# Sums of squares as a rounded pair, tiles turned by transposes, and a rearranged start in a ten-block transformer kernel

## The reference

```python
def norm_mod(h, j):
    shift = mod[:, j, 0][:, None, :]
    scale = mod[:, j, 1][:, None, :]
    return _rms(h) * g_norm[l, j] * (1.0 + scale) + shift

x = x + 0.5 * gate(0) * _swiglu(norm_mod(x, 0), w_ffn_up[l, 0], w_ffn_down[l, 0])
x = x + gate(1) * _mixer(norm_mod(x, 1), w_in[l], ...)
```

## Time and profile before

| | |
|---|---|
| three runs | 1594.5, 1595.07, 1602.45 us; median 1595.07 |
| profiled execution | 1595.17 us |
| its span, first to last instruction | 1593.2 us |
| busy | TensorE 1559.0 us, VectorE 1285.0, ScalarE 906.3, GpSimd 243.0 |
| mean granted TensorE clock | 0.998 of 2.4 GHz |

### The profile page before, as it was taken

One profiled execution on the slowest core, in us unless ns is written; L12 is line 12 of the kernel. 1 busy time (PEld: TensorE's weight loads), 2 busy tenths in 40 slices (PEclk: granted clock), 3 DMA queues, 4 the chain that ended last, 5 costly groups with the idle time before them and its releaser, 6 DMA issues.

```text
span 1593.2 us, 32431 instructions
## 1 busy us (share of the span) xinstructions
PE 1559.0 (98%) x13288; PEld 1536.6 (96%) x13288; DVE 1285.0 (81%) x1933; ACT 906.3 (57%) x1565; POOL 243.0 (15%) x256
## 2 busy tenths in 40 slices
PE   4999999999999999999999999999999999999998
PEld 3999999999999999999999999999999999999998
DVE  6788898888888888888887898778888889786553
ACT  5455457665554655459664445567555466664553
POOL 4122000022210222000112231001221010021100
PEclk9999999999999999999999999999999999999999
DMA  9999974559998899864569998434999973457761
GB/s 347 338 339 331 328 272 158 160 188 348 310 318 280 290 306 322 308 222 151 185 224 340 311 317 288 159 115 147 311 333 339 317 235 121 142 188 238 240 213 41
DMA packets 110996, 403.11 MB, mean 253 GB/s; under 512 B 12562, under 2 KB 12818, under 8 KB 110720
## 3 DMA queue, kind: packets, MB, share of 16 engines
q1 hardware_dynamic: 109280, 395.87, 72.0%
q0 software_dynamic: 1568, 5.17, 1.1%
HBM read 399.94 MB, written 1.05 MB: 252 GB/s over the span
## 4 chain that ended last, share of the span: by engine, by line
PE 87%; DVE 8%; ACT 2%; DMA 1%; issue 1%; SPq 0%; DVEq 0%; ACTq 0%
PE PS L557 86%; DVE SCR L1692 2%; DVE WL L1689 2%; DMA ring<-in_ada 1%; DVE SCR L1689 1%; DVE ring L1715 1%; ACT WH L1211 1%; DVE SCR L2046 1%; DVE SMALL L2045 1%; DVE SMALL L2084 0%; ACT SCR L1497 0%; PE PS L1050 0%; DVE SCR L1686 0%; DVE MOD L1686 0%; ACT HH L1243 0%
## 5 line engine op out<-in xcount | busy, mean ns | idle before, releaser
L1689 DVE TENSOR_TENSOR WL<-ring,WH 128x1024 fp32r<-128x1024 f32 (+1 forms) x508 | 603.9, 1222 | 186.4 <-ACT WH L1211 186.1
L557 PE MATMUL PS<-HH,WH 128*128 128x256 f32 (+1 forms) x2640 | 629.0, 280 | 2.2 <-ACT WH L1211 2.2
L557 PE MATMUL PS<-HL,WH 128*128 128x256 f32 (+1 forms) x2640 | 614.9, 277 | 0.0
L1211 ACT ACTIVATE WH<-ring 128x1024 fp32r<-128x1024 f32 (+1 forms) x508 | 511.0, 1049 | 44.3 <-PE PS L557 42.3
L557 PEld LDWEIGHTS PS<-HH,WH 128*128 128x128 f32 x2640 | 496.7, 188 | 3.3 <-ACT WH L1211 2.3
L557 PEld LDWEIGHTS PS<-HL,WH 128*128 128x128 f32 x2640 | 491.6, 188 | 0.6
L557 PE MATMUL PS<-HH,WL 128*128 128x256 f32 (+1 forms) x2640 | 375.9, 278 | 0.8 <-DVE WL L1689 0.6
L1715 DVE CUSTOM_DVE_ANT_0 ring<-ring,CB,VC 128x1024 f32<-128x1024 f32 x238 | 331.0, 1407 | 11.3 <-DMA ring<-in_ada 11.3
L557 PEld LDWEIGHTS PS<-HH,WL 128*128 128x128 f32 x2640 | 337.1, 189 | 1.6 <-DVE WL L1689 1.6
L557 PE MATMUL PS<-AH,WH 128*128 128x256 f32 x1056 | 291.9, 276 | 0.0
L557 PE MATMUL PS<-AH,WL 128*128 128x256 f32 x1056 | 291.6, 276 | 0.2 <-DVE WL L1689 0.2
(11 more groups left out here) (215 smaller groups left out, 1474.9 us busy)
## 6 DMA issues: line engine op xcount, KB each, us to landing
ring<-in_up SPq DMA_DIRECT2D x176, 512.0 KB, 5.5
ring<-in_ada SPq DMA_DIRECT2D x144, 512.0 KB, 6.1
ring<-in_ffn SPq DMA_DIRECT2D x132, 512.0 KB, 4.8
ring<-in_mod SPq DMA_DIRECT2D x96, 512.0 KB, 5.9
ring<-in_down SPq DMA_DIRECT2D x88, 512.0 KB, 5.9
ring<-in_win SPq DMA_DIRECT2D x64, 512.0 KB, 5.5
ring<-in_wout SPq DMA_DIRECT2D x32, 512.0 KB, 4.2
ring<-in_winv SPq DMA_DIRECT2D x8, 512.0 KB, 4.4
```

Of the source, the lines that this page charges most:

```text
L557: return e.matmul(out, lhsT, rhs, start=start, stop=stop, skip_group_check=skip)
L1211: e.activation(half_of(i)[0], slot_of(("half", i, 0))[:, 0:w], ACT.Copy).then_inc(s_hi, 1)
L1689: return e.tensor_tensor(out, a, b, op)
```

## The change

- **Squares.** GpSimd now adds all eight squares (seven steps). ScalarE rounds the sum into `SH`, GpSimd writes the remainder into `SL` (both lie where chunks 0 and 1 of `SQ` were), and TensorE sums over partitions by two fp32r products with rounded ones (`onesr`). They stand behind `early(n, 1)` instead of inside `early(n, 0)`. On ScalarE one ring half, rounded after R before, is rounded before Ln.
- **Tiles.** VectorE scales the tile itself in place (`unit_rows`, 128x256) instead of the identity, and TensorE turns it by two transposes.
- **c.** The first transfer into `CB` is gone; TensorE turns the eight columns of silu(c), each spread over 128 columns, into PSUM, and ScalarE copies the result into `CB`. The second c is still a transfer.
- **Start.** Eight fp32 products of X by the identity, whose result nobody reads, stand before the first weight product.
- **Mixer 1.** `stick_weights(1)` stands before `hi(u0 + 11)`.

```diff
 def square_sums(m):
-    for c in range(1, KD - 1):
+    for c in range(1, KD):
         e.wait_ge(s_sq, 8 * m - 7 + c)
         if c > 1:
-            e.wait_ge(s_psum, 6 * m + c - 7)
+            e.wait_ge(s_psum, 7 * m + c - 8)
         e.tensor_tensor(SQ[:, c, :], SQ[:, c - 1, :], SQ[:, c, :], ALU.add).then_inc(s_psum, 1)
+    e.wait_ge(s_sqh, m)
+    e.tensor_tensor(SL[:, :], SQ[:, KD - 1, :], SH[:, :].bitcast(F32), ALU.subtract).then_inc(s_sql, 1)
 ...
 def sum_squares(m):
-    e.wait_ge(s_psum, 6 * m)
+    e.wait_ge(s_sql, m)
     if m > 1:
         e.wait_ge(s_r, m - 1)
-    mm(PS[:, 6, 0:256], ones, SQ[:, KD - 2, :], start=True, stop=False)
-    e.wait_ge(s_sq, 8 * m)
-    mm(PS[:, 6, 0:256], ones, SQ[:, KD - 1, :], start=False, stop=True).then_inc(s_ss, 1)
+    mm(PS[:, 6, 0:256], onesr[:, :], SH[:, :], start=True, stop=False)
+    mm(PS[:, 6, 0:256], onesr[:, :], SL[:, :], start=False, stop=True).then_inc(s_ss, 1)
 ...
     if p == 0:
-        sum_squares(n)
         k = KD - 1
 ...
     last.then_inc(s_half, 1)
+    if p == 1:
+        sum_squares(n)
 ...
-        last = mm(PS[:, turn_bank(n, o), 256 + 128 * c:384 + 128 * c], OT[o % 4][:, 128 * c:128 * c + 128], DG[o % 2])
+        last = e.transpose(PS[:, turn_bank(n, o), 256 + 128 * c:384 + 128 * c], OT[o % 4][:, 128 * c:128 * c + 128], ident1)
 ...
 e.wait_ge(s_const, 16)
+e.wait_ge(s_cc, 1)
+for k in range(KD):
+    last = e.transpose(PS[:, k // 4, 128 * (k % 4):128 * (k % 4) + 128], vec("c", k).to_broadcast([128, 128]), ident)
+last.then_inc(s_cspread, 1)
 e.wait_ge(s_xload, 16)
 ...
 last.then_inc(s_flip, 1)
+for c in range(8):
+    mm(PS[:, 6, 0:256], ident, X[:, c % KD, :])
 ...
 def norm(m):
+    e.wait_ge(s_psum, 7 * m)
+    e.activation(SH[:, :], SQ[:, KD - 1, :], ACT.Copy).then_inc(s_sqh, 1)
+    hi_half(2 * UNIT0[m] + 3)
     e.wait_ge(s_ss, m)
     step(e.activation(R[:, :], PS[:, 6, 0:256], ACT.Ln, bias=eps, scale=1.0 / D))
     e.activation(R[:, :], R[:, :], ACT.Exp, scale=-0.5).then_inc(s_r, 1)
-    hi_half(2 * UNIT0[m] + 3)
 ...
                 tile_scale(n, o0 + 1)
+                stick_weights(1)
                 hi(u0 + 11)
-                stick_weights(1)
 ...
-e.wait_ge(s_cload, 16)
-e.activation(CB[:, :], CB[:, :], ACT.Silu).then_inc(s_cb, 1)
 lnexp()
+e.wait_ge(s_cspread, 1)
+e.activation(CB[:, :], PS[:, 0:2, :].rearrange("p a s -> p (a s)"), ACT.Copy).then_inc(s_cb, 1)
 ...
-def diagonal(n, o):
+def unit_rows(n, o):
+
     e.wait_ge(s_oss, o + 1)
-    if o >= OUT0[n] + 2:
-        e.wait_ge(s_ot, o - 1)
-    ts(DG[o % 2], ident1, SM_[:, 114 + o % 2:115 + o % 2], None, ALU.mult, None).then_inc(s_od, 1)
+    ts(OT[o % 4], OT[o % 4], SM_[:, 114 + o % 2:115 + o % 2], None, ALU.mult, None).then_inc(s_od, 1)
```

More of the change, by code:

```diff
@@ L181, in vec @@
             return VC[:, VEC[name] + i:VEC[name] + i + n]
-        ident, ones, bd, ntri, partner, rev, causal, nones = (const(n) for n in (
-            "ident", "ones", "bd", "ntri", "partner", "rev", "causal", "nones"))
+        ident, bd, ntri, partner, rev, causal, nones = (const(n) for n in (
+            "ident", "bd", "ntri", "partner", "rev", "causal", "nones"))
         eps = const("eps")
-        ident1 = identr[:, :].bitcast(F32)
+        ident1, ones1 = identr[:, :].bitcast(F32), onesr[:, :].bitcast(F32)
         one = const("one")
@@ L279, in build @@
         JK = scr(256)
-        DG = [scr(128) for _ in range(2)]
         Scratch.at = 0
@@ L872, in recurrence_sums @@
                     for k in range(4):
-                        last = mm(PS[:, 7, 0:256], ones, GT[:, k, :], start=k == 0, stop=k == 3)
+                        last = mm(PS[:, 7, 0:256], ones1, GT[:, k, :], start=k == 0, stop=k == 3)
                     last.then_inc(s_gnss, 1)
@@ L986, in latent_sums @@
                             mm(PS[:, 6, 256 + t:257 + t], MSQ[:, k, 128 * t:128 * t + 128], one, start=k == 0, stop=k == 1)
-                    mm(PS[:, 6, 0:256], ones, MSQ[:, 2, :]).then_inc(s_mss, 1)
+                    mm(PS[:, 6, 0:256], ones1, MSQ[:, 2, :]).then_inc(s_mss, 1)
                 def keys():
@@ L1992, in mixer1 @@
                 share(n, 2)
-                diagonal(n, o0)
-                diagonal(n, o0 + 1)
+                unit_rows(n, o0)
+                unit_rows(n, o0 + 1)
                 lo(u0 + 11)
@@ L2005, in mixer1 @@
                 partial(n, 3)
-                diagonal(n, o0 + 2)
-                diagonal(n, o0 + 3)
+                unit_rows(n, o0 + 2)
+                unit_rows(n, o0 + 3)
                 lo_half(2 * u0 + 24)
@@ L2178, in mixer2 @@
                 tile_rest(n, o0 + 2)
-                diagonal(n, o0 + 4)
+                unit_rows(n, o0 + 4)
                 gates(n)
@@ L2189, in mixer2 @@
                 partial(n, 1)
-                diagonal(n, o0 + 5)
+                unit_rows(n, o0 + 5)
                 maxima2(a0 + 5, 1)
@@ L2195, in mixer2 @@
                 tile_rest(n, o0 + 4)
-                diagonal(n, o0 + 6)
+                unit_rows(n, o0 + 6)
                 partial(n, 3)
@@ L2202, in mixer2 @@
                 tile_rest(n, o0 + 5)
-                diagonal(n, o0 + 7)
+                unit_rows(n, o0 + 7)
                 partial(n, 5)
```

28 lines of the change are left out of this document (15 added, 13 removed).

## The result

| | changed | before |
|---|---|---|
| median of 15 runs each | 1604.54 us | 1596.53 us |
| lowest and highest | 1594.09, 1614.59 | 1593.82, 1604.05 |
| ratio of the changed kernel to before | 1.0047, 95% interval 1.0029 to 1.0065 | |
| profiled execution, its span | 1606.41, 1604.6 us | 1595.17, 1593.2 us |

The forecast was 1589.8 with a range up to 1594.0: it failed, on the side of slower. Besides the median, the spread is to be noted: 20 us between runs of one and the same changed kernel, 10 us before.

What follows compares the result with a forecast made beforehand. TensorE, busy 98% of the span, was taken to bound the kernel; gains of 1.7 (start), 1.4 (boundaries), 0.6 and 1.7 (mixers) sum to 5.4 us, so 1595.2 - 5.4 = 1589.8 us, range 1583.5 to 1594.0.

Steps and rivals of the forecast that it cites:

- What bounds the kernel: Whole kernel: TensorE is busy 98% of the span, so time falls only where its queue gets shorter or waits less.
- A wait also costs some 0.1 on the next spacing.: At the boundaries: besides its 0.3 us length, TensorE's wait adds some 0.1 us to the step after it.
- The start: Before and in the first half-column: first weight product still at 34.65, its 24 products faster, gain 1.7 us.
- The clock part: At the start: clock at 2.4 GHz, so the first half-column's 24 products take 2.75 us instead of 4.45.
- the prediction's rule that transposes do not count as work for the clock: At the start: the eight new transposes warm nothing for TensorE's clock; the real products do; no change in time.
- The boundary: Nine sub-block changes: 0.63 us saved each, 0.2 left after waits; 1.4 us at seven, -0.15 each at two.
- The spare of the sum: At the boundary: the sum's input is ready at 329.5, TensorE arrives at 330.26, 0.7 us spare; 2 after an FFN.
- rival (c): At nine boundaries the sum's input SL comes too late; every microsecond costs 9, 1607.8 at 2 us; chance 0.06.
- Mixers: Mixer ends, tiles turned by transposes: 0.3 us gained per first-type mixer, 0.85-0.9 per second-type; 0.6 and 1.7 in all.
- (a): Whole kernel: all savings count, other engines are never late; 13.4 us gained, so 1581.8; chance 0.15.
- (b): At the start: no gain, as transfers are not sooner or the clock drops; 1591.5 to 1593; chance 0.2.
- four signs of being wrong: TensorE waiting for SL; no gap before the eighth product; clock 0.50 after 31; VectorE idle above 0.5 us before early products.

Runs made afterwards that it cites:

- f1: The changed kernel run again with nothing edited: median 1597.03 us of eleven runs, one of 4037.51 standing apart; ratio 1.0004.
- e7: The kernel before with three chained, unread VectorE instructions ahead of the remainders of h at each boundary: 1611.85 us, ratio 1.0098.
- e9: e5's kernel with c spread by a transfer again, without the eight transposes: 1593.19 us, +1.3.
- e10: e5's kernel without the eight unread products by the identity: 1593.2 us, +1.3.
- e2: The changed kernel with one 256-column product given as two of 128 in each sub-block after the first: 1596.36 us, ratio 0.9985.
- e5: The changed kernel with two split products (256 columns as 128 and 128) in every FFN, twelve in all: 1591.91 us, ratio 0.9962.
- f3: e1's kernel with two split products in sub-block 0 and two 258-column products in each of the other five FFNs: 1598.45 us, ratio 0.9996.
- e12: e4's kernel with the twelve split products of e5: 1593.0 us, +1.1 to e5.
- e3: The kernel before with one unread VectorE instruction of 0.4 us ahead of the remainders of h at each boundary: 1596.33 us, ratio 0.9999.
- e4: The changed kernel with the squares, their sum and its place as before: 1590.71 us, ratio 0.9972.
- e8: The kernel before with the twelve split products of e5: 1597.92 us, ratio 1.0001.
- e1: The changed kernel with the squares summed by one plain fp32 product inside the second early half-column, without SH and SL: 1599.86 us, ratio 1.0011.

## Why the prediction was wrong

Point by point:

- **What bounds the kernel.** Right: TensorE at 98%, its queue alone counts. But I took the time of a product as a constant, 0.114 us. This is the step that failed, and it is in no single term: every term of the sum multiplies or subtracts at that one rate. In the profile of after 1463, 1483 and 1034 products of sub-blocks 2, 3 and 5 run in the slower rhythm, at 0.00444 us each: 17.7 us. Without them 1606.4 - 17.7 = 1588.7, 1.1 us under the forecast; the lowest runs of f1 (1589.4 and 1590.1) lie there too.
- **"A wait also costs some 0.1 on the next spacing."** The restart was mis-sized. Its visible part is right (the last HL product is followed after 0.22 instead of 0.11). Its hidden part is a chance of 4.5 ns on each of up to 1500 products behind it, 6.5 us. At FFN boundaries with such waits and no split, five of fifteen were slow behind the wait (after 3, f1 1, e7 1); two of these five (sub-block 3 of after, 9 of f1) had come to it slow, from the step to 256 columns.
- **The signs were there.** One of three runs of before was 7.4 us above the others (1602.45 against 1594.5 and 1595.07), and I did not ask what in one program can take 7 us more with nothing changed.
- **The start.** 1.7 predicted, 3.05 measured at the second half-column (36.04 against 39.10 in the earlier trace rows), from two errors of opposite sign. The clock part held in kind (granted 1.00) but was sized too high: the first half-column took 3.2 us instead of 4.45, not 2.75, as four of its steps are of 0.22 to 0.25; that is 1.25. The other 1.8, for which the prediction had nothing, is that the first weight product starts at 32.84 and not at 34.65. The products ahead of it were through sooner than worked out: the unread ones began at 29.39, not 31.2, since x landed 1.9 us sooner (not 1.3) and the turns of x took 4.38 us instead of 5.38:

```profile
20.46 4.38 PE L1162 MATMUL PS<-CN,SCR 128*128 128x128 f32 x24 [3.73 <-ACT X L1637]
```

Up to 23.51 these turns follow each other at 0.213, from 23.70 on at 0.109, and 23.68 is where the changed kernel's first clock record (1.00) stands. Nothing but transposes had run on TensorE by then, so the prediction's rule that transposes do not count as work for the clock is not borne out here. (Ahead of a trace's first clock record the clock column prints 1.00 all the same, as in the earlier trace rows from 10 to 20; the rate is to be read there from the steps, 0.213.) In the medians of e9 and e10 the two parts of the start are worth 1.3 us each.
- **The change from the plain to the rounded products at the start** is a new place for a draw, which I did not have: of the twelve profiles with the unread products four began slow (f1 and e2, which stayed so, e5 and f3, which a split led out).
- **The boundary.** Predicted: the eighth HL product waits 0.3, net gain 0.2. Measured: the seventh waits too, the three steps are 0.23, 0.39 and 0.22 where 0.11 is due, so 0.5 lost instead of 0.4; ahead of the first mixers five steps are long and 1.1 is lost. Net about 1.0 us for all nine (e12 against e5, product by product, less the start and sub-block 5), against 1.4 - 0.3 predicted. The spare of the sum was 0.2 us (SL ends at 326.70, TensorE comes at 326.90), not 0.7, since GpSimd's remainder took 1.66 us and not 1.0 to 1.2, so rival (c) was closer than its price had it; behind the FFNs, where the remainder took 1.15, the spare was 1.8, as predicted.
- **Mixers.** Right: the wait before the third tile is 0.7 (row `DVE SQ L1699`), the second mixers gain 0.84 and 0.90 from the tiles. A turn takes 0.11 us, so the Trainium skill's factor of 4 (TensorE: Matmul & The Clock Gate, Terms) is not what this trace has, which is 2.
- **Rivals and range.** None of the rivals had this mechanism; (a) and (b) were about where 1588.7 would fall, not about what came on top. The chance of 0.05 for slower by over 0.5% rested on (c) alone. None of the four signs of being wrong came (no wait for SL, a gap at the eighth product, the clock at 1.00 after 31, no idle VectorE ahead of the first early product at 224.4): they watched the terms of the sum, and none the rate of the ordinary products.

What stays open: why there are two rhythms. They are not the granted clock (1.00 in both) and no wait stands in them; nor do they look like traffic (the DMA share is the same within 0.05, and f3 turns the rhythm from one product to the next). Two more columns once toggle it and a product in two pieces nearly always has the quick one behind it, which looks like a phase between two things in TensorE or its queue that uniform work never shifts; that is argued, not shown. Nor was it found why the step from 258 to 256 columns led to the quick rhythm at all nine boundaries of before, e3, e4 and e8, but not at all of e1's and of the changed kernel's (it failed at 3, 4 and 9 there, so the "nine times of nine" in e2's expectation was wrong for that kernel). And what moved the changed kernel by 7.5 us from its first set to f1 is open.

## What to carry to other kernels

Where one engine runs uniform instructions for 100 us and more, count them per window: two counts at the same clock and no wait are a second rhythm, and runs that fall into evenly spaced groups are its sign. A wait in front of such a stretch is then priced by the stretch behind it and not by its own length; in these kernels a broken product or two behind each wait or change of form (0.12 us each) was a cheap insurance and made differences of about 1 us readable. Judge a small change only with the rhythm held still: the changed kernel gave 1.0047 and 1.0004 without the splits, 0.9962 with them.

## What the runs showed of the hardware that I had not expected

- fp32r products of 256 columns with their weight loads follow each other at 0.1133 or 0.1178 us, at a granted clock of 1.00 in both.
- The rhythm can hold over 1500 products and differs from one execution of a program to the next (sub-blocks 2, 3, 5 slow in one profile of the changed kernel, 0 and 9 in the other).
- One product of 258 columns among those of 256 toggled it ten times of ten.
- GpSimd's passes over 128x256 vary: the remainder SL took 1.66 us at four boundaries and 1.15 at the other five, its additions 0.82 on the mean of 63.
- TensorE's steps halved from 0.213 to 0.109 us at 23.7, and the clock record of 1.00 stands there, with nothing but transposes before it (the changed kernel; the same at 22.9 in e10 and 25.5 in e9).
